# Inverting the delta rule's triangular blocks in 32x32 corners, four side by side, instead of 64x64 blocks, two side by side

## The reference, cut to what matters

```
A = jnp.where(strict, jnp.einsum("bhncd,bhnsd->bhncs", kb, kc) * decay, 0.0)
rhs = jnp.concatenate([vc * bc[..., None], kb * jnp.exp(gc)[..., None]], axis=-1)
sol = lax.linalg.triangular_solve(A, rhs, left_side=True, lower=True, unit_diagonal=True)
u, w = sol[..., :Dv], sol[..., Dv:]
```

## Time and profile before

| | |
|---|---|
| median of 3 runs | 2746.93 us (2744.68 to 2751.48) |
| the profiled execution | 2750.94 us, of which the span is 2749.2 us |
| PE busy | 2705.3 us, 98% of the span |
| DVE, ACT, POOL busy | 76%, 46%, 2% |
| granted TensorE clock, mean | 0.995 of full |

### The profile page before, as it was taken

One profiled execution on the slowest core, in us unless ns is written; L12 is line 12 of the kernel. 1 busy time (PEld: TensorE's weight loads), 2 busy tenths in 40 slices (PEclk: granted clock), 3 DMA queues, 4 the chain that ended last, 5 costly groups with the idle time before them and its releaser, 6 DMA issues.

```text
span 2749.2 us, 52010 instructions
## 1 busy us (share of the span) xinstructions
PE 2705.3 (98%) x20739; PEld 2372.3 (86%) x20748; DVE 2091.8 (76%) x3771; ACT 1265.3 (46%) x1926; POOL 56.9 (2%) x89
## 2 busy tenths in 40 slices
PE   9999999999999999999999999999999999999998
PEld 7887898886998689998999998886999999999886
DVE  6766887766775569999666667885999976666787
ACT  4534554433553444455444445442555444444543
POOL 0010000020000000000000000000000000000000
PEclk9999999999999999999999999999999999999999
DMA  5305884314883135643555557663564355555764
GB/s 212 108 34 230 320 325 151 110 41 190 329 329 140 68 129 191 231 150 114 187 193 185 184 192 259 241 232 129 188 230 166 116 177 191 183 185 193 248 243 170
DMA packets 95348, 515.07 MB, mean 187 GB/s; under 512 B 18384, under 2 KB 24912, under 8 KB 38352
## 3 DMA queue, kind: packets, MB, share of 16 engines
q1 hardware_dynamic: 74256, 485.11, 48.9%
q10 hardware_dynamic: 20928, 27.63, 2.9%
HBM read 494.88 MB, written 17.83 MB: 186 GB/s over the span
## 4 chain that ended last, share of the span: by engine, by line
PE 81%; DVE 16%; issue 1%; ACT 1%; DMA 0%; POOL 0%; DVEq 0%; ACTq 0%; SPq 0%; POOLq 0%
PE bank L917 19%; PE bank L905 19%; PE bank L944 12%; PE bank L2089 8%; DVE ring_r L2671 3%; PE bank L2345 3%; PE bank L730 3%; PE bank L581 2%; PE bank L789 2%; PE bank L2363 1%; DVE sb L2754 1%; DVE sb L2745 1%; PE bank L659 1%; DVE sb L2746 1%; PE bank L560 1%
## 5 line engine op out<-in xcount | busy, mean ns | idle before, releaser
L2089 PE MATMUL bank<-peer_pass_high,q_high 128*128 128x256 f32 x1232 | 356.4, 289 | 1.3 <-DVE ring_r L2705 0.8
L2089 PE MATMUL bank<-h_low,q_high 128*128 128x256 f32 x1232 | 347.7, 282 | 0.0
L2089 PE MATMUL bank<-peer_pass_high,ring_r 128*128 128x256 f32 x1232 | 347.1, 282 | 0.0
L917 PE MATMUL bank<-peer_pass_high,peer_pass_hidden 128*128 128x512 f32 x1024 | 339.5, 393 | 0.0
L905 PE MATMUL bank<-peer_pass_high 128*128 128x256 f32 x1008 | 283.2, 281 | 0.0
L905 PE MATMUL bank<-peer_pass_high,ring_r 128*128 128x256 f32 x1008 | 282.9, 281 | 0.0
L905 PE MATMUL bank<-hT_r,peer_pass_high 128*128 128x256 f32 x1008 | 282.9, 281 | 0.0
L1023 DVE TENSOR_TENSOR ring_r<-ring,peer_pass_high 128x1024 fp32r<-128x1024 f32 x128 | 156.8, 1225 | 155.2 <-ACT peer_pass_high L1663 155.2
L2089 PEld LDWEIGHTS bank<-peer_pass_high,q_high 128*128 128x128 f32 x1232 | 233.8, 190 | 1.9 <-DVE ring_r L2705 1.0
L2089 PEld LDWEIGHTS bank<-peer_pass_high,ring_r 128*128 128x128 f32 x1232 | 233.4, 189 | 0.0
L2089 PEld LDWEIGHTS bank<-h_low,q_high 128*128 128x128 f32 x1232 | 232.7, 189 | 0.0
(11 more groups left out here) (431 smaller groups left out, 6324.0 us busy)
## 6 DMA issues: line engine op xcount, KB each, us to landing
ring<-in_experts SPq DMA_DIRECT2D x256, 1024.0 KB, 4.8
ring<-in_w SPq DMA_DIRECT2D x137, 1024.0 KB, 4.8
sb<-in_w_mod SPq DMA_DIRECT2D x48, 1024.0 KB, 6.7
sb<-spill SPq DMA_DIRECT2D x64, 256.0 KB, 5.0
spill<-sb ACTq DMA_DIRECT2D x20, 512.0 KB, 6.5
spill<-sb ACTq DMA_DIRECT2D x48, 128.0 KB, 1.9
sb<-in_ln ACTq DMA_DIRECT2D x8, 512.0 KB, 6.8
sb<-in_post ACTq DMA_DIRECT2D x4, 512.0 KB, 4.6
```

Source lines behind the costliest of these rows:

```text
L917: m = pe.matmul(ps[4 + 2 * tb + half][:, :], g[:, t], w, start=False, stop=False, skip_group_check=True)
L2089: m = pe.matmul(out, l, r, start=start and i == 0, stop=stop and i == 2)
```

## The change: what it does, and the diff

The inverse is formed only up to blocks of 32. Every 64x64 matrix has two 32x32 diagonal corners, so the two matrices of a pair have four, one in each quarter of the partitions. The new `corners` (which stands for `products`) multiplies 32x32 by 32x32: for each of the 12 pairs of a direction, four matmuls, one for each quarter, all into one bank. A stage is thus two calls (one for each direction `dr`) of 48 matmuls in place of four calls of 12. Merges remain for 16 and 32, and the stacks that hold the corners are half as wide.

The last merge is done by block products: `z` multiplies the off-diagonal block of A by one corner's inverse, ACT copies it negated, and `inv` writes the whole 64x64 result into a bank with three matmuls for each matrix (two corners transposed back by a product with `eye`, and the off-diagonal block). ACT and DVE copy two groups each into `TT`. POOL's twelve scalings are put in the order k for `w`, v, k for the state, and each signals `kv_scaled`; PE waits for 4, 8 and 12 of them before `w`, the first `v` and the first `kv`.

```diff
-    j += [(("at", g), "act") for g in range(GRP)]
+    j += [(("at", dr), "act") for dr in range(2)]
...
-LEVELS = ("m8", "m16", "m32")
+LEVELS = ("m8", "m16")
+HALF = 32
...
-    def products(key, lhsT, rhs, g):
+    def corner(M, m, q):
+
+        cols = slice(q % 2 * HALF, (q % 2 + 1) * HALF) if M.shape[2] == CHUNK else slice(0, HALF)
+        return M[q * HALF:(q + 1) * HALF, m, cols]
+
+    def corners(key, lhsT, rhs, dr):
 
         b = J.give(pe, key, lay)
-        for h in range(GH):
-            for par in range(2):
-                rows = slice(par * 64, par * 64 + 64)
-                r = rhs[rows, rows] if rhs is c["ident"] else rhs[rows, GH * g + h, :]
-                m = pe.matmul(ps[b][rows, h * 64:h * 64 + 64], lhsT[rows, GH * g + h, :], r, start=True, stop=True)
+        for n in range(TB * GH):
+            for q in range(4):
+                rows = slice(q * HALF, (q + 1) * HALF)
+                r = rhs[rows, rows] if rhs is c["ident"] else corner(rhs, dr * TB * GH + n, q)
+                m = pe.matmul(ps[b][rows, n * HALF:(n + 1) * HALF], corner(lhsT, dr * TB * GH + n, q), r, start=True, stop=True)
         m.then_inc(J.filled, 1)
...
+    J.evac(pe, ("tyt", len(LEVELS) - 1, 1), lay)
+    for tb in range(TB):
+        b = J.give(pe, ("z", tb), lay)
+        for h in range(GH):
+            for dr in range(2):
+                mat = (dr * TB + tb) * GH + h
+                for par in range(2):
+                    far, near = (slice((2 * par + half) * HALF, (2 * par + half + 1) * HALF) for half in (1 - dr, dr))
+                    m = pe.matmul(ps[b][near, h * HALF:(h + 1) * HALF], k.A[far, mat, dr * HALF:(dr + 1) * HALF], k.TT_h[far, mat, :],
+                                  start=True, stop=True)
+        m.then_inc(J.filled, 1)
+    eye = k.cc["eye"]
+    for g, (dr, tb) in enumerate(groups()):
+        J.evac(pe, ("z", tb), lay)
+        b = J.give(pe, ("inv", g), lay)
+        for h in range(GH):
+            mat = g * GH + h
+            for par in range(2):
...
+                pe.matmul(ps[b][far, h * CHUNK:(h + 1) * CHUNK], k.T_h[far, mat, :], eye[far, :], start=True, stop=True)
+                pe.matmul(ps[b][near, own], k.T_h[near, mat, :], eye[near, dr * HALF:(dr + 1) * HALF], start=True, stop=True)
+                m = pe.matmul(ps[b][near, other], k.T_h[near, mat, :], k.Z_h[near, tb * GH + h, :], start=True, stop=True)
+        m.then_inc(J.filled, 1)
+    for g in range(2, GRP):
+        J.evac(pe, ("inv", g), lay)
+    wait(k.kv_scaled, 4)
...
+    for dr in range(2):
+        J.evac(v, ("at", dr), lay)
+        v.tensor_tensor(halves(k.DT_h, dr), halves(k.AT_h, dr), half_mask("half_d8_m8", 0), ALU.mult).then_inc(k.D_ready.sem, 1)
...
+    for g in range(0, GRP, 2):
+        copy(("inv", g), k.TT[:, GH * g:GH * g + GH, :], lambda t: shaped(t[:, 0:BLOCKS], GH, CHUNK))
...
+    for src, dst, f in ((k.Kn, k.kbg, k.beg), (k.Vn, k.vb, k.beta), (k.Kn, k.kdec, k.ekd)):
+        for dr in range(2):
+            for tb in range(TB):
+                p.tensor_tensor(shaped(dst[:, dr, tb, :], GH, HD), shaped(src[:, tb, :], GH, HD),
+                                bc(f[:, tb, dr * GH:(dr + 1) * GH].unsqueeze(2), GH, HD), ALU.mult).then_inc(k.kv_scaled.sem, 1)
```

More of the change, by code:

```diff
@@ L741, in pe_layer @@
             m.then_inc(J.filled, 1)
[L743 to L746, removed]
+    for dr in range(2):
+        wait(k.D_ready, dr + 1)
+        corners(("d2", dr), k.DT_h, k.DM, dr)
+        corners(("d2t", dr), k.DM, k.DT_h, dr)
     wait(k.P0_ready)
[L748 to L755, removed]
-    for lv in range(len(LEVELS)):
[L757 to L766, removed]
+    for dr in range(2):
+        J.evac(pe, ("d2t", dr), lay)
+        corners(("d4", dr), k.D2T_h, k.D2_h, dr)
+        corners(("p1t", dr), k.D2_h, k.TT_h, dr)
+    for dr in range(2):
+        J.evac(pe, ("p1t", dr), lay)
+        corners(("t", dr), k.TT_h, k.E4_h, dr)
+        corners(("tt", dr), k.E4_h, k.TT_h, dr)
+    for lv in range(len(LEVELS)):
+        wait(k.LT_ready, lv + 1)
+        for dr in range(2):
+            J.evac(pe, ("t", dr) if lv == 0 else ("ty", lv - 1, dr), lay)
+            corners(("y", lv, dr), k.LT_h[lv], k.T_h, dr)
+        for dr in range(2):
+            J.evac(pe, ("tt", dr) if lv == 0 else ("tyt", lv - 1, dr), lay)
+            J.evac(pe, ("y", lv, dr), lay)
+            corners(("ty", lv, dr), k.TT_h, k.Y_h, dr)
+            corners(("tyt", lv, dr), k.Y_h, k.TT_h, dr)
         if lv == 0:
@@ L801, in pe_layer @@
             wait(k.state_zeroed)
+            wait(k.kv_scaled, 8)
         else:
@@ L1335, in dve_layer, with accumulate @@
     wait(k.P0_ready)
[L1337 removed]
+    def accumulate(key, M, dr, op):
         b = J.take(v, "dve", key, lay)
[L1339 removed]
+        v.tensor_tensor(halves(M, dr), halves(M, dr), shaped(ps[b][:, 0:BLOCKS], TB * GH, HALF), op).then_inc(J.read["dve"], 1)
+    for dr in range(2):
+        b = J.take(v, "dve", ("d4", dr), lay)
+        v.tensor_tensor(halves(k.E4_h, dr), half_mask("half_m16_eye", 1), shaped(ps[b][:, 0:BLOCKS], TB * GH, HALF), ALU.add)\
          .then_inc(J.read["dve"], 1)
[L1342 to L1351, removed]
+        accumulate(("p1t", dr), k.TT_h, dr, ALU.add)
+    for lv, (name, i) in enumerate((("half_d8_m8", 1), ("half_m16_eye", 0))):
+        v.tensor_tensor(k.LT_h[lv], k.AT_h, half_mask(name, i, MATS), ALU.mult).then_inc(k.LT_ready.sem, 1)
     for lv in range(len(LEVELS)):
[L1353 removed]
+        J.evac(v, ("tt", 1) if lv == 0 else ("tyt", lv - 1, 1), lay)
         if lv == 0:
@@ L1357, in dve_layer @@
             v.tensor_tensor(od, od, bc(k.onorm[:, :].unsqueeze(2), 12, HD), ALU.mult).then_inc(k.od_ready.sem, 1)
[L1358 to L1363, removed]
+        for dr in range(2):
+            accumulate(("ty", lv, dr), k.T_h, dr, ALU.subtract)
+            accumulate(("tyt", lv, dr), k.TT_h, dr, ALU.subtract)
+    for g in range(1, GRP, 2):
+        b = J.take(v, "dve", ("inv", g), lay)
+        v.tensor_copy(part(k.TT, g), shaped(ps[b][:, 0:BLOCKS], GH, CHUNK)).then_inc(J.read["dve"], 1)
     J.evac(v, "cv", lay)
@@ L1588, in act_layer, with corners @@
     out_head(DH - 1)
[L1589 to L1593, removed]
+    def corners(key, M, dr):
+        copy(key, M[:, dr * TB * GH:(dr + 1) * TB * GH, :], lambda t: shaped(t[:, 0:BLOCKS], TB * GH, HALF))
+    for dr in range(2):
+        corners(("at", dr), k.AT_h, dr)
     for name, dst in (("kn", k.Kn), ("vn", k.Vn)):
```

88 lines of the change are left out of this document (43 added, 45 removed).

## The result

| | before | changed |
|---|---|---|
| median, in the same comparison | 2745.8 us (2743.51 to 2751.48, 4 runs) | 2837.82 us (2836.32 to 2841.57, 4 runs) |
| profiled span | 2749.2 us | 2839.8 us |
| PE busy | 2705.3 us, 98% | 2714.7 us, 96% |
| granted clock, mean | 0.995 | 0.966 |

The change makes the kernel slower: the ratio is 1.0334, 95% interval 1.0315 to 1.0353, or +92 us.

What follows compares the result with a forecast made beforehand. PE, busy 98%, bounds the kernel, its instruction supply nearly equal to its arithmetic. Stage +40.2 us and clock 1 us, for two layers, give +82 us: 2829 us against the median, range 2790 to 2852 us.

Steps and rivals of the forecast that it cites:

- The supply decides: In the inverse's stage, PE's instruction blocks of 256 set the time, 23.4 blocks instead of 12.1: +40.2 us a layer; 0.76.
- the signs: Changed profile: bursts of about 128 pairs started by "issue", 142 packets, stage 86 to 91 us, all else unchanged.
- The length of a round: In the stage, PE gets one block of 256 instructions every 3.9 us, between 3.8 and 3.96.
- The parts of a round: Instruction fetch for PE: 1.2 us until it starts, transfer 1.2 to 1.6 us, 1.4 us until usable.
- (b): A round gets shorter when blocks run out faster: 2.8 us, +16 us a layer, 2778 us; 0.07 together with (c).
- The clock: Low clock slows `w` and the first projection behind the stage: 1 us a layer, bounds 0 to 3.5.
- Waits at nothing: PE's waits for ACT or DVE between stages are covered by the supply: nothing; without that cover 2.3 us a layer.
- POOL at nothing: POOL's scalings end 24 us ahead of `w`, so counting them one by one is worth nothing.
- (a): Instruction supply is no limit in the stage: -15 us a layer, 2717 us; 0.08.
- (c): A deeper instruction store, eight blocks at the stage's start instead of one: +13 us a layer, 2775 us; 0.07 with (b).
- (d): A least distance of 25 ns between small matmuls in the stage: +30 us a layer, 2807 us; 0.04.
- (e): The clock stays low through the scan behind the stage: more than 3.5 us a layer on top, over 2840 us; 0.05.

Runs made afterwards that it cites:

- pad_full: The kernel before with two idle one-column matmuls behind each one of `products`, 2880 instructions more per layer: 2829.22 us, ratio 1.0289.
- corners_loop: The changed kernel, each `corners` call running 5 pairs of matrices twice in a run-time loop, then 2 once, pairs 6 to 10 left out: 2790.32 us, ratio 1.0144.
- corners_wide: The changed kernel with most `corners` matmuls streaming two neighbouring corners, 64 columns instead of 32, in as many instructions: 2833.16 us, ratio 1.0308.
- scaled_only: The kernel before with only POOL's twelve scalings in the new order, each counted, and PE's three waits: 2749.66 us, ratio 1.0004.
- turns_on_dve: The kernel before with DVE turning 32x32 blocks instead of PE computing the transposed twins, 16 of 60 calls: 2739.86 us, ratio 0.996.

## Why the prediction was right, point by point

**The supply decides: shown.** The predicted bursts, their start by "issue", ACT and DVE waiting for PE, and 142 packets are all in the trace. Two of the signs were a little off: layer 1's stage of 91.3 us is just outside the 86 to 91 us, and not all else kept its length (+4.5 us ahead of and between the stages). `pad_full` makes the loss without a corner, `corners_loop` takes half of it away with as many matmuls executed, `corners_wide` doubles the columns at no cost.

**The length of a round.** I took 3.9 us. From 134.86 to 214.77 us lie 21 rounds: 3.80 us each, and without the long one 3.74. So the rounds alone took 79.9 us where mine would have taken 81.9. The stage is nevertheless longer than my 88.1 us (89.8 and 91.3), because I left 6.2 us for what stands around them and it is 9.9: 2.2 us ahead of 134.86, where I had counted the first blocks as there, and 7.7 us behind 214.77, a last round and then `w` at the low clock (0.72 us of wait and 2.84 us) for which I had 0.7. In layer 1 the long round of 6.6 us comes on top. The mis-sized term of the sum is the stage: +42.0 and +42.7 us instead of +40.2. That it came out so near is in part luck: in layer 0 the round was 2.0 us too long over 21 rounds and what stands around the rounds 3.7 us too short, and the two errors partly cancel.

**The parts of a round.** My split into 1.2 us, a transfer of 1.2 to 1.6 us and 1.4 us came from stretches cut too coarsely. Cut at 0.4 us around the burst that starts at 163.62, the one stretch of four in which the queue moves anything holds a whole packet (41 GB/s times 0.4 us is 16.4 KB):

```profile
164.00:164.40 0.40, 0.40 (x47) 0.40 (x43) 0.00 (x0) 0.00 (x0) 0.00 (x0) 0.50 0.00 0
164.40:164.80 0.40, 0.40 (x48) 0.40 (x40) 0.00 (x0) 0.07 (x1) 0.00 (x0) 0.50 0.15 41
164.80:165.20 0.40, 0.40 (x48) 0.40 (x43) 0.00 (x0) 0.40 (x1) 0.00 (x0) 0.50 0.00 0
```

So the transfer lies between 0.8 and 1.2 us after the start of the burst, takes 0.4 us at most, and 2.4 us or more pass until the next burst at 167.17. The start of the packet and the whole (3.55 us in this round) were about right; the transfer was put too long and the time behind it too short. The floor of 2.6 us that I gave rival (b) was added up from these wrong parts; from the start of the packet to the next burst this round has 2.4 to 2.8 us, so its size holds by luck.

**The clock.** I took 1 us a layer for `w` and the first projection together, between bounds of 0 and 3.5. It is 2.4 and 1.6 us: `w` takes 2.84 us instead of 1.63 in both layers (this part lies in the stage as measured here), the first projection 3.17 and 2.37 us instead of 1.99 and 1.98. So this term was mis-sized too, inside its bounds. That the low clock costs little between the bursts held: rounds at or near half the clock (3.74 and 3.77 us in the two layers of the change) lie among those of the other kernels nearer to the full one (3.63 to 3.86 us).

**Waits at nothing, POOL at nothing: held.** PE waits 0.7 us for a consumer in layer 0; `scaled_only` is at 1.0004.

**The rivals.** (a) and (b) fell with the rounds: the bursts are over in 1.3 to 1.9 us and PE stands still for the rest, with rounds of 3.74 us where (b) had 2.8. A small part of (b) may be true: the two rounds with bursts of 1.3 and 1.4 us (from 138.26 and 141.72) take 3.46 and 3.58 us, those of before, with 3.72 us of matmuls, 3.96. No run separates this from the scatter of single rounds, 3.3 to 4.3 us. (c) fell since the breaks begin with the first burst. (d) fell with 9.4 ns a pair. (e) fell with the clock of 1.00 from 225 us on in layer 0 and from 693 us on in layer 1. Against its own profiled execution the total came 8.6 us above the forecast (2841.57 for 2833): 4.3 from the stage, and 4.5 from what stands ahead of it and between the layers.

## What to carry to other kernels

Count a stage's instructions, not only its matmul time: a float32 matmul is four of them here, and in this kernel PE gets a block of 256 in 3.5 to 3.9 us on average, so instructions that need less than 14 to 15 ns each wait, however small the tiles are. Breaks of "issue" that stand 128 pairs apart, and one packet of the instruction queue for each, are the sign; a stage that shows the first of them had nothing to win here from smaller and more parallel tiles. What can help is fewer instructions to bring in. Two ways were tried: a run-time loop (`corners_loop`, 16 packets fewer, though with a price of its own), and work that another engine does in one instruction where PE needs 48 (`turns_on_dve`). `corners_wide` suggests a third, a wider operand in one matmul, since twice the columns cost nothing; no run used it to save instructions.

## What the runs showed of the hardware that was not expected

- A round of the supply hardly depends on what PE executes: its mean over eight or more rounds is 3.63 to 3.86 us with 32x32 and 64x64 matmuls and with those of one column. Tensor DMAs beside it stretch it to 5.1 and 6.6 us.
- From 160 to 180 us the granted clock is 0.50 in the change (32 moving columns, PE's records cover 10.9 us of the 20) and 1.00 in `corners_wide` (64 columns, 10.3 us); elsewhere in its stage `corners_wide` is granted less too.
- Instructions that a loop of 80 instructions repeats bring no new packets (126 instead of 142).
- Four quarters in turn take a weight load and a matmul of 32x32 every 9.4 ns at the full clock, 14.1 ns at half of it.
